# Panel loads, first picks and opening order of a one-layer decoder kernel with an expert gather

## What is computed

```
h = rmsnorm(x);  proj = h @ w_in          # q/k/v of 12 dilated + 8 MoBA heads, 2 gates
x += (sig(g_a) * (dilated @ w_a) + sig(g_b) * (moba @ w_b)) @ w_out
x += cross_attention(rmsnorm(x), rmsnorm(mem))         # 4 heads of 128
q  = rmsnorm(x) @ w_q;  scores = q . sub_keys          # 8 heads x 2 x 128 keys
top 16 of the sums of the two top-16 lists -> 16 experts per head and token
x += sum_e softmax(top)_e * gelu(h . u[e]) * v[e];   y = rmsnorm(x)
```

## Time and profile before

| | |
|---|---|
| runs | 992.87, 994.3, 989.75 us (median 992.87) |
| the profiled execution | 996.5 us, span 994.6 us |
| mean granted TensorE clock | 0.967 |
| PE busy | 826.6 us (83%) |
| DVE busy | 685.2 us (69%) |
| POOL busy | 339.8 us (34%) |
| ACT busy | 261.7 us (26%) |
| gathers (queue q0) | 268.45 MB, 64.9% of 16 DMA engines |
| panels and the rest from SP (queue q1) | 55.61 MB, 17.2% |
| read from HBM | 322.77 MB |

### The profile page before, as it was taken

The page is one execution under the profiler, slowest core; times in us unless marked ns, Lnnn a source line. Parts: engine busy times, 40 slices in busy tenths (PEclk is TensorE's granted clock), DMA queues, the critical chain, the costliest instruction groups (busy, mean ns, idle before and its releaser), DMA issues.

```text
span 994.6 us, 11330 instructions
## 1 busy us (share of the span) xinstructions
PE 826.6 (83%) x3604; PEld 517.3 (52%) x3604; DVE 685.2 (69%) x1710; ACT 261.7 (26%) x481; POOL 339.8 (34%) x300
## 2 busy tenths in 40 slices
PE   5989879999998889989889787777777777777776
PEld 5989768899976635535435232223323223232232
DVE  4334763465565878887888777777877877777665
ACT  6435363454554422112122011110110101101012
POOL 0000173013000444554465444444445434544310
PEclk9999889999999989999999999999999999999989
DMA  8987322354441799999999999999999999999993
GB/s 289 201 189 230 121 85 86 120 220 169 149 169 43 303 422 421 420 422 420 420 421 420 422 421 422 421 422 421 422 422 422 422 422 422 422 422 422 421 422 155
DMA packets 48802, 324.87 MB, mean 327 GB/s; under 512 B 5508, under 2 KB 8824, under 8 KB 10104
## 3 DMA queue, kind: packets, MB, share of 16 engines
q0 software_dynamic: 36864, 268.45, 64.9%
q1 hardware_dynamic: 11752, 55.61, 17.2%
q10 hardware_dynamic: 144, 0.26, 0.1%
HBM read 322.77 MB, written 1.54 MB: 326 GB/s over the span
## 4 chain that ended last, share of the span: by engine, by line
DMA 44%; PE 34%; DVE 8%; issue 7%; ACT 4%; POOL 2%; DVEq 0%; POOLq 0%; SPq 0%
DMA late_ring<-in_experts,expert 37%; PE y L781 8%; PE ps L561 7%; PE ps L562 7%; PE ps L563 7%; DMA arena<-in_experts,expert 4%; DMA raw<-in_panels 3%; DVE w_lo L1140 2%; POOL arena L1556 1%; DVE diag L1432 1%; ACT w_hi L846 1%; DVE row_max L1206 1%; POOL late_ring L1556 1%; PE ps L661 1%; PE ps L649 1%
## 5 line engine op out<-in xcount | busy, mean ns | idle before, releaser
L781 PE MATMUL y<-arena,diag 128*128 128x512 f32 x536 | 249.9, 607 | 61.1 <-DVE diag L1432 60.9
L781 PE MATMUL y<-late_ring,diag 128*128 128x512 f32 x472 | 230.6, 630 | 65.2 <-DVE diag L1432 65.2
L1556 POOL DMA_INDIRECT arena<-in_experts,expert x135 | 155.5, 1152 | 252.7 <-PE y L781 141.2
L1440 DVE CUSTOM_DVE_ANT_0 arena<-arena 128x1024 f32<-128x1024 f32 x135 | 165.2, 1224 | 77.4 <-DMA arena<-in_experts,expert 77.2
L781 PEld LDWEIGHTS y<-arena,diag 128*128 128x128 f32 x536 | 98.5, 192 | 205.0 <-DVE diag L1432 102.9
L1556 POOL DMA_INDIRECT late_ring<-in_experts,expert x121 | 138.8, 1147 | 168.8 <-PE y L781 135.4
L781 PEld LDWEIGHTS y<-late_ring,diag 128*128 128x128 f32 x472 | 90.6, 199 | 196.8 <-DVE diag L1432 99.2
L1440 DVE CUSTOM_DVE_ANT_0 late_ring<-late_ring,arena 128x1024 f32<-128x1024 f32 x121 | 147.7, 1222 | 51.3 <-DMA late_ring<-in_experts,expert 48.3
L1023 ACT ACTIVATE acts<-dots 128x2 f32<-128x2 f32 x126 | 25.7, 204 | 519.5 <-DVE dots L1440 519.4
L1140 DVE TENSOR_TENSOR w_lo<-raw,w_hi 128x2048 fp32r<-128x2048 f32 x42 | 98.2, 2341 | 86.0 <-ACT w_hi L846 86.0
L561 PE MATMUL ps<-h_hi,w_hi 128*128 128x256 f32 x400 | 119.5, 299 | 3.2 <-DVE w_lo L1140 2.8
(11 more groups left out here) (208 smaller groups left out, 942.9 us busy)
## 6 DMA issues: line engine op xcount, KB each, us to landing
raw<-in_panels SPq DMA_DIRECT2D x43, 1024.0 KB, 4.9
arena<-line_scratch SPq DMA_DIRECT2D x8, 320.0 KB, 11.7
arena<-in_experts,expert POOLq DMA_INDIRECT x135, 30.1
arena<-in_panels SPq DMA_DIRECT2D x2, 1024.0 KB, 7.5
late_ring<-in_experts,expert POOLq DMA_INDIRECT x121, 30.2
x<-in_x SPq DMA_DIRECT2D x2, 512.0 KB, 3.8
arena<-in_mem SPq DMA_DIRECT2D x1, 1024.0 KB, 8.9
late_ring<-in_panels SPq DMA_DIRECT2D x1, 1024.0 KB, 8.9
```

Of the source, the lines that this page charges most:

```text
L781: mm = pe.matmul(y[:, t, half * 512:(half + 1) * 512], diag[:, s % DIAGS, :], row[:, at:at + 512], start=False, stop=False, skip_group_che ...
L1440: i = nc.vector.tensor_tensor_reduce(row, row, h_rows[:, t, :], 1.0, 0.0, ALU.mult, ALU.add, dots[:, s:s + 1])
L1556: nc.gpsimd.indirect_dma_start(out=slot(u, s), out_offset=None, in_=experts, in_offset=bass.IndirectOffsetOnAxis(ap=expert[:, parity, s:s ...
```

## The change

Six edits. (1) Panel qpeer2 is loaded over tile 1's scores, behind kv2, and qpeer7 into buffer 1, behind qpeer1, after the last `cross_o`; the raw ring counts only the panels that go through it (`RAW_LOADED`), so qpeer3 waits for qpeer0's split and qpeer4 for qpeer1's. (2) Buffer 8 takes the place of buffer 1 at the start, and buffers 10 and 11 are free behind qpeer0's last product. (3) The first unit's picks are made in two halves of 8 experts (`route_first`); POOL may issue the first eight gathers after the first half. (4) Cross output 1 goes ahead of query (1,0), and `start_output(1)` goes ahead of the cross-attention transposes. (5) "line" and "keys" come behind qkv0, the bias loads behind qkv4, 5, 7, 8, 9, 11, 12, 13, and mem's load behind qkv14 with its norm at j == 13. (6) ACT evaluates one Sqrt on a spare element before the first squares, behind a memset on POOL, and tile 0's `rows_rstd` is ahead of qpeer1's split on DVE.

```diff
-BIAS_AFTER = [f"qkv{4 + a}" for a in range(P // LINE_COPIES)]
+BIAS_AFTER = [f"qkv{j}" for j in (4, 5, 7, 8, 9, 11, 12, 13)]
+MEM_AFTER = "qkv14"
+MEM_NORM_AT = 13
...
-OWN_PLACE_OVER = 2
+OWN_PLACE_OVER = 1
...
-LOADED_EARLY = {"qpeer5": 6, "qpeer6": 7, "qpeer7": 8}
-EARLY_BEHIND = {"kv0": "qpeer5", "kv1": "qpeer6", "qpeer2": "qpeer7"}
-FIRST_BUFFERS = [0, 1, 2, 3, 4, 5, 9, 10, 11, 12, 13]
-JOINS = {48: 6, 64: 7, ALL_FROM + 5: 8, ALL_FROM + 6: 14, ALL_FROM + 7: 15}
+OVER_SCORES = "over_scores"
+LOADED_EARLY = {"qpeer2": OVER_SCORES, "qpeer5": 6, "qpeer6": 7, "qpeer7": 1}
+EARLY_BEHIND = {"kv0": "qpeer5", "kv1": "qpeer6", "kv2": "qpeer2", "qpeer1": "qpeer7"}
+RAW_LOADED = [name for name in PANELS if name not in LOADED_EARLY]
+FIRST_BUFFERS = [0, 8, 2, 3, 4, 5, 9, 10, 11, 12, 13]
+JOINS = {48: 6, 64: 7, ALL_FROM + 5: 1, ALL_FROM + 6: 14, ALL_FROM + 7: 15}
...
-    add("line", "dve")
-    add("keys", "act")
     for j in range(15):
         add(f"qkv{j}", "act")
+        if j == 0:
+            add("line", "dve")
+            add("keys", "act")
...
     query(0, 0)
+    cross_output(1)
     query(1, 0)
-    cross_output(1)
...
             def load_panel(n):
-                if n >= RAW_RING:
-                    sp.wait_ge(w_lo_ready, n - RAW_RING + 1)
-                sp.dma_start(raw[:, n % RAW_RING, :], panels[n]).then_inc(panel_in[n % RAW_RING], 16)
+                i = RAW_LOADED.index(PANELS[n])
+                if i >= RAW_RING:
+                    sp.wait_ge(w_lo_ready, PANELS.index(RAW_LOADED[i - RAW_RING]) + 1)
+                sp.dma_start(raw_panel(n), panels[n]).then_inc(panel_in[i % RAW_RING], 16)
...
-                    last_use = "ocross1_1" if early == "qpeer7" else f"probs_t{SELF_HEADS - 1}"
+                    last_use = f"cross_o{CROSS_HEADS - 1}" if early == "qpeer7" else f"probs_t{SELF_HEADS - 1}"
...
             start_output(0)
+            start_output(1)
...
+            act.wait_ge(spare_set, 1)
+            nc.scalar.activation(spare[:, 0:1], spare[:, 0:1], ACT.Sqrt)
             squares("mix", x)
...
-                if j == 1:
+                if j == MEM_NORM_AT:
                     act.wait_ge(mem_loaded, 16)
...
             for j in range(15):
                 pace(f"qkv{j}")
-                if j == 1:
+                if j == 0:
+                    dve.wait_ge(small_in, 16 * SMALL)
+                    b = take("line")
+                    took(nc.vector.tensor_tensor(line[0:SELF_HEADS], b[0:SELF_HEADS, 0:LINE_PAD],
+                                                 line_mask[0:SELF_HEADS], ALU.add))
+                if j == MEM_NORM_AT:
                     normalise("mem", mem_rows, mem_rows)
...
+                nc.vector.tensor_reduce(expert_f[:, best], pick[:, best], AX.X, ALU.add)
+                equal(rest).then_inc(route_step, 1)
+                after_step(0, 13)
+                nc.vector.tensor_copy(expert[:, 0, best], expert_f[:, best]).then_inc(first_experts_ready, 1)
+                times_pairs(rest).then_inc(route_step, 1)
+                after_step(0, 14)
+                nc.vector.tensor_reduce(expert_f[:, rest], pick[:, rest], AX.X, ALU.add).then_inc(picks_summed, 1)
+                dve.wait_ge(picks_summed, 1)
+                nc.vector.tensor_copy(expert[:, 0, rest], expert_f[:, rest]).then_inc(experts_ready, 1)
...
-                pool.wait_ge(experts_ready, u + 1)
                 for s in range(TOPK):
                     n = u * TOPK + s
+                    if n == 0:
+                        pool.wait_ge(first_experts_ready, 1)
+                    elif s == (TOPK // 2 if u == 0 else 0):
+                        pool.wait_ge(experts_ready, u + 1)
...
                     if n == FIRST_BUFFERS.index(10):
+                        pool.wait_ge(product_ready, PLACE["qpeer0_1"] + 1)
+                    if n == FIRST_BUFFERS.index(12):
                         pool.wait_ge(product_ready, PLACE["qpeer1_1"] + 1)
```

More of the change, by code:

```diff
@@ L344, in build @@
         g_ffn_row = part(11264, D)
-        g_final_row = raw[:, (len(PANELS) - 2) % RAW_RING, 0:D]
+        g_final_row = raw[:, RAW_LOADED.index("qpeer4") % RAW_RING, 0:D]
         LATE = [2 * SPLIT_RING, 2 * SPLIT_RING + 1] + [
-            i * SPLIT_RING + j for j in range(SPLIT_RING) if j != LAST_PLACE for i in range(2)] + [
-            i * SPLIT_RING + LAST_PLACE for i in range(2)]
+            i * SPLIT_RING + j for j in (PLACE_OF["qpeer0"], PLACE_OF["qpeer1"], LAST_PLACE) for i in range(2)]
         def at_buffer(b):
@@ L388, in raw_panel @@
             name = PANELS[n]
-            return at_buffer(LOADED_EARLY[name]) if name in LOADED_EARLY else raw[:, n % RAW_RING, :]
+            if name not in LOADED_EARLY:
+                return raw[:, RAW_LOADED.index(name) % RAW_RING, :]
+            place = LOADED_EARLY[name]
+            return scores[:, PEER_HEADS * 2 * PEER_KEYS:] if place == OVER_SCORES else at_buffer(place)
         ps = ctx.enter_context(nc.psum_tensor("ps", [P, BANKS, 512], F32))
@@ L440, in build @@
         experts_ready = sem("experts_ready")
+        first_experts_ready = sem("first_experts_ready")
+        picks_summed = sem("picks_summed")
         slot_in = [sem(f"slot_in{i}") for i in range(BUFFERS)]
@@ L614, in _ @@
             turn("mix", mix_xn)
-            pe.wait_ge(small_in, 16 * SMALL)
-            nb = rel_bias.shape[0]
-            b = begin("line")
-            pe.matmul(b[0:SELF_HEADS, 0:LINE_PAD], rel_sb[0:nb], onehot[0:nb],
-                      start=True, stop=True).then_inc(product_ready, 1)
-            b = begin("keys")
-            for p in range(2):
-                mm = pe.transpose(b[:, p * P:(p + 1) * P], keys_rows[:, p, :], ident[:])
-            mm.then_inc(product_ready, 1)
             for j in range(15):
@@ L629, in _ @@
                     channels_by_tokens(f"qkv{j}", h_pair, "mix" if j == 0 else None)
+                if j == 0:
+                    pe.wait_ge(small_in, 16 * SMALL)
+                    nb = rel_bias.shape[0]
+                    b = begin("line")
+                    pe.matmul(b[0:SELF_HEADS, 0:LINE_PAD], rel_sb[0:nb], onehot[0:nb],
+                              start=True, stop=True).then_inc(product_ready, 1)
+                    b = begin("keys")
+                    for p in range(2):
+                        mm = pe.transpose(b[:, p * P:(p + 1) * P], keys_rows[:, p, :], ident[:])
+                    mm.then_inc(product_ready, 1)
             all_taken("qkv14")
@@ L798, in _ @@
             query(0, 0)
+            cross_output(1)
             query(1, 0)
-            start_output(1)
-            cross_output(1)
             turn_rows(1)
@@ L893, in _ @@
             turned("mix", h_hi, CHUNKS)
-            b = take("keys")
-            took(nc.scalar.copy(keysT[:].rearrange("p a b -> p (a b)"), b[:, 0:2 * P]))
             for j in range(15):
                 pace(f"qkv{j}")
-                if j == 1:
+                if j == MEM_NORM_AT:
                     act.wait_ge(mem_loaded, 16)
@@ L903, in _ @@
                 took(copy_qkv(nc.scalar.copy, j, b, qT, kT, vv))
+                if j == 0:
+                    b = take("keys")
+                    took(nc.scalar.copy(keysT[:].rearrange("p a b -> p (a b)"), b[:, 0:2 * P]))
             act.wait_ge(half_b_ready, 1)
@@ L1317, in _ @@
             rows_mean(0)
+            rows_rstd(0)
             split_panel(PANELS.index("qpeer1"))
-            rows_rstd(0)
             STEPS = 14
```

58 lines of the change are left out of this document (51 added, 7 removed).

## The result

The changed kernel took 1003.71 us (median of 4 runs, 1002.62 to 1005.46), the kernel before 992.7 in the same series: a ratio of 1.0116, 95% interval 1.0088 to 1.0144, or 11.0 us slower. The forecast was 7.3 us and 1000.2. Its profiled execution took 1004.17 us, its span 1002.1, against 994.6 before.

A forecast was written before the change was run, and what follows sets the result against it. Full DMA engines behind 330 us, with waits for free buffers, were taken to bound it. Opening +4 and back end +3.3 (4.6 late, 1.3 returned) gave +7.3 on 992.9: 1000.2 us; range 988 to 1004, the forecast's own 997 to 1004.

The forecast's parts named there:

- The DMA term of -1.3: Gather: panels out return 2.2 us before the twelfth gather, less 0.9 us dry later; net -1.3.
- The picks in halves: First unit's picks: first gather 1.8 us earlier against its scores, but buffers bound the stretch; worth 0.
- The opening: Qkv panels: waits for splits of 6.7 us against 2.8; +3.9, rounded to +4, bounds -4.9 to +6.5.
- The chain through SP's wait: Opening: the line's write moves from 16.82 to 23.4, panel 3's cast from 25.58 to 30.7, and what follows is later.
- Panels 9 and 10 get the slow transfers instead, 1 us: Opening: these panels now load beside the moved bias transfers; 1 us of PE's waits.
- The back end: Cross output to slot 0: 2.9 us later queries plus 1.7 for half clock; slot 0 4.6 us late.
- scores (1,0) at 328.9 (322.3 + 5.5 + 1.1): Back end: query (1,0)'s scores behind the moved cross output and start_output(1); then cast to 332.6, query (2,0) at 334.9.
- The half clock behind it: PE after its idle stretch from 330.6: 3.4 us at half clock, costing 1.7 us (bounds 0 and 1.7).
- Bytes decide: Rival, gather: the panels' 7.5 us return in full if slot 0 is free before 356.5; 985.4, chance 0.2.
- the rule of the Trainium skill: Gather: variable DMA time is bytes over 436 GB/s; 3.1 MB less are 7.2 us less, end near 985.7.
- Opening gains: Rival: spread bias loads feed every panel in time, -4.9, back end costs 1.6; 989.6, chance 0.15.
- Both small: Rival: the opening recovers (+1), the back end costs +1.6; 995.5, chance 0.21.

The follow-up runs named there:

- e4: The changed kernel with opening, cross output order and picks as before, keeping the panels in front of the gather; 991.42 us, ratio 0.9992.
- e13: The changed kernel with PE waiting for ACT's copies alone ahead of a query's transposes and its key scores; 1005.45 us, ratio 1.0125.
- e14: e13 with ACT also splitting qpeer2 ahead of the copies of query (1,0); 999.99 us, ratio 1.0086.
- e15: The changed kernel with only ACT's split of qpeer2 moved ahead of the copies of query (1,0); 1000.79 us, ratio 1.0073.
- e9: e4 with ACT's first gelu ahead of the last two heads' scores of tile 1; 988.11 us, ratio 0.9941.
- e7: The changed kernel with PE waiting for ACT's copy alone ahead of a query's transposes; 1006.1 us, ratio 1.0127.
- e8: The kernel before with ACT's first gelu ahead of the last two heads' scores of tile 1; 995.22 us, ratio 1.0007.
- e3: The changed kernel with the first unit's picks in one piece, as before; 1006.08 us, ratio 1.0143.
- e1: The changed kernel with the opening as before: "line" and "keys", bias loads and mem's load in their old places; 1000.59 us, ratio 1.0093.
- e5: The changed kernel with only "line" and "keys" ahead of qkv0 again; 1000.03 us, ratio 1.0061.
- e6: The changed kernel with start_output(1) back right ahead of cross output 1; 1004.59 us, ratio 1.0116.
- e16: The changed kernel with "line" and "keys" ahead of qkv0 and e14's two edits, keeping the new cross order; 989.84 us, ratio 0.9975.

## Why the prediction came out as it did

**Right.** The direction and the mechanism. The panels' time was not returned, since slot 0 was late and the engines ran dry. The DMA term of -1.3 was measured as -1.3 in the tail and -0.8 in the median of e4. The picks in halves are worth nothing, mem's and the bias loads cost nothing, and `start_output(1)` 1.5 us (1.1 forecast, bounds 0 and 1.88). The first gather came 9.35 us behind the scores (forecast 9).

**The opening was undersized: +4 forecast, 5.5 measured.** The chain through SP's wait was right. The sum of waits after was right too (6.7 forecast, 6.5 the mean), but by luck: ahead of qkv8 the forecast had 5.7 and the eight kernels 2.4 to 4.2 (mean 3.1); behind it the forecast had 1 and they had 3.5. The term "Panels 9 and 10 get the slow transfers instead, 1 us" was too small, and why the panels behind qkv8 come late was not tried. What it was set against failed as well: the 2.8 us of waits before came from one execution, and the five with that opening have a mean of 2.1. "line" and "keys" cost what was forecast, 0 (1.2 less 1.2). Some 1.1 us are assigned to nothing.

**The back end was undersized: +4.6 forecast; 8.4 measured, 6.9 in the slot 0 stretch and some 1.5 ahead of it.** The step that failed is "scores (1,0) at 328.9 (322.3 + 5.5 + 1.1)". It followed ACT's list and PE's work, but not what PE waits for: the transposes of query (1,0) wait until all copies so far are done, and with the cross output in front these include DVE's rows of tile 1, behind the whole of the picks. That is the 3.35 us on PE's line. The forecast put the end of scores (1,0) 11.0 us behind the scores of (0,0) (328.9 less 316.85 and 1.1) and query (2,0) 17.0; they came after 14.6 and 20.5. e13 shows that taking half of this wait away moves the cast by 2.3 us and slot 0 by 1.3. The rest of the chain, the cast behind the softmax, was the forecast's own and is shown by e14 and e15. The half clock behind it was taken as 3.4 us long, and was 13.7 (0.50 from 329.2 to 342.9). The length cost little more than forecast: from query (2,0) to the twelfth issue it took 30.1 us, forecast 30.2 (28.5 before, and 1.7).

**The sum, and why the spans hid the miss.** The forecast span was 1001.9 and the measured one 1002.1, the twelfth issue 8.8 us later where the terms gave 8.6. Yet the median moved by 11.0. The profiled execution of before was 3.6 us above its median, with an opening of 93.6 instead of the 92.3 of its group, and a half clock of 3.4 us near 310. I carried these along as if the change kept them. It did not: its opening waits for a new thing, and the half clock near 310 is not in its trace. By the marks the terms are 5.5 (opening), 1.5 (middle), 6.9 (slot 0) and -1.3 (tail), together 12.6; the medians say 11.0 (8.7 to 14.3 by the interval). That the forecast span came out within 0.2 us is luck: the terms of the opening and the back end were too small, and what was particular to the execution of before made up for it.

**The rivals.** Bytes decide: the rule of the Trainium skill (DMA: Bandwidth & Descriptors, Anatomy of one DMA), with its estimated 7.2 us, did not hold for the change. It nearly does in e9, where no buffer binds: 6.4 us by the spans, 5.9 by the medians. The trace agrees with the rule only where the engines never wait for a buffer. Opening gains: the spread bias loads did not feed the panels in time, since panel 3 was late; with "line" ahead they did (waits 0 to 1.1). Both small: fell with the two sizes above.

**What stays open.** How far PE's wait for DVE alone would go: e7 and e13 moved or halved it, and a kernel without it was not tried; it would need another rule for which product the key scores' bank waits for. And why the single undos return less in the medians than both together; the intervals (some 4 us on a difference) leave room for no effect at all.

## What to carry to other kernels

Where two resources bind in turn (here DMA bytes and a free buffer), each relief alone measures as nothing, and both together pay: e8 1.0007, e4 0.9992, e9 0.9941. Before a step is moved, list who waits for it and what stands behind it in every engine's own list: one moved product made SP issue a panel's load 4.8 us later (24.62 against 19.87), and one moved output made ACT's cast and PE's transposes late, while a single call moved on ACT took most of that away. Set a forecast's sum against several executions, or take out first what is particular to the profiled one.

## What was not expected of the hardware

The granted clock's stretches at 0.50 (1.2 instead of 2.4 GHz) were longer here than the 3.4 us of the earlier trace rows from which the forecast took its length. Around PE's idle time between queries (1,0) and (2,0) it was 0.50 for 13.7 us in the change and in e3, for 10.2 in e1 and e5, and for 6.8 in e6, e7, e13 and e15. In e14, where PE waited only 1.11 us before query (2,0), it was 1.00 for the whole of 320 to 340; in e16, with the same two edits, it was 0.50 for 3.4 us. A half clock in a stretch where PE waits for others costs less than half its length: 13.7 us at 0.50 held 7.3 us of PE work, and half of that, 3.7 us, is the most it can have cost (an estimate).

Panel loads of 1 MB landed at quite different speeds from one execution to the next. Before and e8 have the same code there, and panel 5 was cast at 40.84 in the one and at 36.89 in the other. The eight openings of the changed order differ by 5.2 us. This scatter is as large as each of the terms sought here; the slot 0 stretch and the tail, by contrast, repeat to 0.9 and 1.1 us wherever the order is the same, the gather's panels gone.
